# Memory attention in a decoder step: values products one step later, cached values in the weight ring, decode chain over steps 8 to 16

## The chip, the cores and the metric

The kernel runs on one core of one Trainium2 chip. The metric is the device time of one execution in microseconds. A core has the engines PE (TensorE, matrix products), DVE (VectorE), ACT (ScalarE), POOL (GpSimd) and SP (SyncE, which here only issues transfers). Each engine has its own instruction list and works it off in order; engines meet at semaphores alone. So a wait holds up everything behind it on the same engine.

## What is computed

One step of a hybrid decoder layer, for 512 prompt tokens and 8 sequences with 4 new tokens each (32 decode tokens, 544 columns in all), width 1024, all in fp32. The layer is a mixer (a state space part beside differential attention), then cross-attention into 256 memory tokens, then a SwiGLU FFN. The part that matters here is the cross-attention with 4 heads of 256:

```python
def mem_attend(hn, mk, mv, w_mq, w_mo):
    q = (hn @ w_mq).reshape(b, t, N_MEM_HEADS, MEM_HEAD_DIM)
    s = jnp.einsum("bqhd,bkhd->bhqk", q, mk)
    p = jax.nn.softmax(s * (MEM_HEAD_DIM ** -0.5), axis=-1)
    o = jnp.einsum("bhqk,bkhd->bqhd", p, mv).reshape(b, t, D_MODEL)
    return o @ w_mo
```

It runs twice: for the prompt with keys and values made from `mem_prompt`, and for the decode tokens with `cache_mem_k` and `cache_mem_v`, 8 sequences of 256 x 1024 each, 1 MB per sequence for keys and 1 MB for values.

## The kernel before

**Weights.** Each weight matrix is cut into units of 1 MB (1024 x 256), numbered through the kernel: U_MQ = 21 to 24 is `w_mq`, U_MO = 25 to 28 is `w_mo`, U_FFN = 29. A product is made of three passes on high and low parts, so a unit goes through three two-slot buffers, slot n % 2: SP loads it to `w_raw`, ACT copies the high part to `w_hi` (`split_hi`, waits for the load and for the last product that read unit n - 2), POOL subtracts to `w_lo` (`split_lo`). SP's `ahead(n)` issues all loads up to unit n that are still missing; ACT's `hi_ahead(n)` does the same for the high parts. Each load waits for the low part of unit n - 2.

**The memory stage.** `mem_order` (lines 405 to 419) is one list that PE, ACT and DVE each walk, every engine doing its share of each entry. It has 18 steps. In step n:
- `ma n`: scores of head n // 4 for the token tile n % 4. PE makes four products (L2125), DVE the maximum (L1570, L1571), ACT the exp (L946), DVE the reciprocal and scaling of tile n - 1 (L1553, L1554).
- `mt n-2` (`ma_tail`): PE transposes the tile's weights (L1797), ACT copies them to `m_pT` (L729). Behind the fourth tile of a head, `ma_tail` on PE waits for that copy and makes the head's values product (L2113, eight products of 512 columns), which `mo h` (`ma_out`, L1563) on DVE turns into high and low parts.
- `kt`, `ks` (steps 0 to 8): sixteen blocks of cached keys, each with 8 transposes into PSUM banks 2 and 7, two copies to `dm_kT` on ACT (L954, L956) and 8 small products (L2144).
- the decode chain: `dsm` and `dsc` (softmax on DVE and ACT), `dpt` (transposes, copy to `dm_pT` L1589), `dv 0` and `dv 1` (cached values products for sequences 0 to 3 and 4 to 7, L2159, into banks 2 and 7), `do` (ACT copies them to `dm_o`, L965), `dot` (transposes and four DVE operations).

**Orders around it.** Ahead of `mem_order`, ACT runs `for n_ in range(4): hi_ahead(U_MQ + n_ + 1)`, so up to unit 25; behind it, `hi_ahead(U_MO + 1)`, unit 26. Behind it, PE runs 16 half products of `w_mo` (`half_product`, L1777) in the order of `HALF_ORDER`: four tiles over the first 272 columns, the same four over the last 272 (which hold the decode tokens), then the other four tiles.

**Buffers of the cached keys and values.** Keys 0 to 3 go to `kv_slots` 0 to 3, keys 4 to 7 to `kx_slots`, which lie on `x_hi` and `x_lo` and are free once unit 24's products are done. Values 0 to 3 reuse `kv_slots` 0 to 3, value 4 has slot 4, value 5 slot 5 (the place of `dm_qz`), values 6 and 7 slots 0 and 1 again.

Of the kernel before, what the change touches and what calls it, by code (L numbers as in the profile page):

```python
# [13 lines left out]
F32 = mybir.dt.float32  # L14
# [6 lines left out]
P = 128  # L21
D = 1024
# [9 lines left out]
NMEM, MH, MD = 256, 4, 256  # L32
# [48 lines left out]
def build(nc, A, O):  # L81
# [123 lines left out]
    kv_slots = [at(f"dm_kv{i}", [P, 2, D], F32, C0 + off) for i, off in enumerate((61440, 69632, 77824, 25600, 33792, 86016))]  # L205
    kx_slots = [at(f"dm_kx{i}", [P, 2, D], F32, B0 + i * 8192) for i in range(4)]
    dm_k = kv_slots[:4] + kx_slots
    dm_v = kv_slots[:4] + kv_slots[4:6] + kv_slots[:2]
    mkT = at("mkT", [P, KT, NMEM], F32, C0 + 45056)
    mv_tok = at("mv_tok", [P, 2, D], F32, C0 + 53248)  # L210
    mk_tok = at("mk_tok", [P, 2, D], F32, C0 + 34816)
# [16 lines left out]
    def bank(i):  # L228

        return pall[:, i, :]  # L230
# [172 lines left out]


    mem_order = []
    for n in range(len(MATT) + 2):
        if n < 16:
            mem_order.append(("ma", n))
        if n < 8:
            mem_order.append(("kt", 2 * n))  # L410
            if n:
                mem_order.append(("ks", 2 * n - 1))
            mem_order += [("kt", 2 * n + 1), ("ks", 2 * n)]
        mem_order += {8: [("ks", 15), ("dsm", 0), ("mo", 0)], 9: [("dsc", 0)], 10: [("dpt", 0), ("mo", 1)], 11: [("dv", 0)],
                      12: [("do", 0)], 13: [("dv", 1), ("dot", 0), ("dot", 1)], 14: [("do", 1), ("mo", 2)],
                      15: [("dot", 2), ("dot", 3)], 16: [("mtail", 15)]}.get(n, [])
        if n >= 2:
            mem_order.append(("mt", n - 2))
    mem_order.append(("mo", 3))

    w_loaded = [S("w_loaded0"), S("w_loaded1")]
    w_hi_ready, w_lo_ready = S("w_hi_ready"), S("w_lo_ready")
# [10 lines left out]
    def _(sp_eng):  # L433
# [135 lines left out]
            e.dma_start(dm_k[b][:], mk_view[b]).then_inc(S("kv_in0"), 16)  # L569
        e.wait_ge(S("mk_stored"), 16)  # L570
        e.dma_start(dm_v[4][:], mv_view[4]).then_inc(S("kv_in3"), 16)
        ahead(U_MO + 1)
        e.wait_ge(acc_full, used(U_MO - 1))
        for b in range(4, 8):
            e.dma_start(dm_k[b][:], mk_view[b]).then_inc(S("kv_in1"), 16)
        e.wait_ge(S("dmT_pe"), 16)
        for b in range(4):
            e.dma_start(dm_v[b][:], mv_view[b]).then_inc(S("kv_in2"), 16)
        e.wait_ge(S("dms"), 16)
        e.dma_start(dm_v[5][:], mv_view[5]).then_inc(S("kv_in3"), 16)  # L580
        e.wait_ge(S("dm_pv"), 1)
        for b in range(6, 8):
            e.dma_start(dm_v[b][:], mv_view[b]).then_inc(S("kv_in3"), 16)
        ahead(U_FFN - 3)

        gate = A["w_gate"][0].rearrange("(k p) c -> p k c", p=P)
# [30 lines left out]
    @block.gpsimd  # L617
    def _(pool):
        e = pool

        def split_lo(n, kts, cols, i=None, per=0):

            off = 0 if i is None else i * per
            e.wait_ge(w_hi_ready, off + (n + 1))
            w = kts * cols
            e.tensor_tensor(w_lo[:, n % 2, 0:w], w_raw[:, n % 2, 0:w], w_hi[:, n % 2, 0:w].bitcast(F32), ALU.subtract)\  # L626
                .then_inc(w_lo_ready, 1)

        e.memset(c_out[:], 0.0).then_inc(S("zeroed"), 1)
        e.memset(c_pad[:], 0.0).then_inc(S("zeroed"), 1)  # L630
        e.wait_ge(S("xs_ready"), 5)
        e.memset(b_pad[:], 0.0).then_inc(S("zeroed"), 1)

        e.wait_ge(w_lo_ready, U_MQ + 1)
        for n in range(U_MQ + 1, U_FFN):
            split_lo(n, *units[n][1:])
        e.wait_ge(w_lo_ready, U_FFN + 1)
        with e.Fori(0, PAIRS - 1) as i:
            for s_ in range(1, 3):
                split_lo(U_FFN + s_, KT, 256, i, 2)  # L640
        for n in range(U_DOWN + 1, N_UNITS):
            split_lo(n, DOWN_K[(n - U_DOWN) % 3][1], 256)
# [3 lines left out]
    def _(act):  # L646
# [294 lines left out]
        for kind, n in mem_order:  # L941
            if kind == "ma":
                e.wait_ge(S("ma_max"), n + 1)
                if n >= 4:
                    e.wait_ge(S("ma_pT"), n - 3)
                e.activation(m_p[:, n % 4, :], bank(4 + n % 2)[:, 0:NMEM], ACT.Exp, scale=MD ** -0.5,  # L946
                             bias=small[:, 28 + n % 4:29 + n % 4], accum_out=small[:, 32 + n % 4:33 + n % 4]).then_inc(S("ma_exp"), 1)
            elif kind == "mt":
                ma_tail(n)
            elif kind == "kt":  # L950
                e.wait_ge(S("dmT_pe"), 2 * n + 1)
                if n >= 2:
                    e.wait_ge(S("dms"), n - 1)
                e.activation(dm_kT[n % 2][:, 0:2, :], bank(2).rearrange("p (a b) -> p a b", a=2), ACT.Copy).then_inc(S("dmT_out"), 1)  # L954
                e.wait_ge(S("dmT_pe"), 2 * n + 2)
                e.activation(dm_kT[n % 2][:, 2:4, :], bank(7).rearrange("p (a b) -> p a b", a=2), ACT.Copy).then_inc(S("dmT_out"), 1)  # L956
            elif kind == "dsm":
                e.wait_ge(S("dm_max"), 1)
                for t in range(2):
                    e.activation(dm_p[:, t, :], bank(3)[:, t * NMEM:(t + 1) * NMEM], ACT.Exp, scale=MD ** -0.5,  # L960
                                 bias=small[:, D_NM + t:D_NM + t + 1], accum_out=small[:, D_L + t:D_L + t + 1]).then_inc(S("dm_exp"), 1)
            elif kind == "do":
                e.wait_ge(S("dm_pv"), n + 1)
                for g in range(2):
                    e.activation(dm_o[:, n, g * 512:(g + 1) * 512], bank((2, 7)[g]), ACT.Copy).then_inc(S("dmo_out"), 1)  # L965
# [31 lines left out]
                e.wait_ge(*n4_add_after((n - 4) // 8, (n - 4) % 8))  # L997
            e.activation(q4_half[:, n % 4, :], yT[:, k, in_half(a)], ACT.Square, scale=D ** -0.5).then_inc(S("norm_sq"), 1)

        hi_ahead(U_MO + 1)  # L1000
        for i in range(13):
            evac_half(i)
            if i == 3:
# [740 lines left out]
    def _(pe):  # L1744
# [355 lines left out]
        def ma_tail(n):  # L2100
            h, i = MATT[n]
            e.wait_ge(S("ma_p"), n + 1)
            if n >= 1:
                e.wait_ge(S("ma_pTo"), n)
            transposes(bank(6), [m_p[:, n % 4, k * P:(k + 1) * P] for k in range(2)]).then_inc(S("ma_pT"), 1)
            if i == 3:
                e.wait_ge(S("ma_pTo"), n + 1)
                for d in range(2):
                    if 0 < h < 3:
                        e.wait_ge(S("ma_o"), 2 * (h - 1) + d + 1)  # L2110
                    for k in range(2):
                        c = (2 * h + d) * P
                        ins = mm(bank(d if h < 3 else 4 + d), mv_tok[:, k, c:c + P], m_pT[:, k, :], start=k == 0, stop=k == 1)  # L2113
                    ins.then_inc(S("ma_pv"), 1)


        e.wait_ge(S("mk_tok_ready"), 4)
        for kind, n in mem_order:
# [7 lines left out]
                ins.then_inc(S("ma_s"), 1)  # L2126
            elif kind == "mt":
                ma_tail(n)
            elif kind == "kt":
                t, k = n // KT, n % KT  # L2130
                if k == 0:
# [34 lines left out]
                    e.wait_ge(S("dmx"), 2 * n)  # L2166
                transposes(bank(3), [dm_o[:, t, k * P:(k + 1) * P] for k in range(4 * half, 4 * half + 4)]).then_inc(S("dmoT"), 1)

        e.wait_ge(S("dmx"), 8)
        def sum_half(out, name, a):  # L2170

            e.wait_ge(*counted(name, "add", 7 * (a + 1)) if name == "n4" else counted("n3", "add", 14 if a else half_adds(11)))
# [13 lines left out]
        def during_mo(i):  # L2186

            def at_k(k):
                if i == 0:
                    e.wait_ge(S("ma_o"), max(6, k + 1))  # L2190
                if (i, k) == (12, 4):
                    sum_half(bank(4), "n3", 0)
                if (i, k) == (13, 2):
                    rows_half(bank(4), "n3", 0)
            return at_k
# [108 lines left out]
```

## Time and profile before

| what | value |
|---|---|
| median of 3 runs | 1030.5 us (1030.44 to 1030.97) |
| the profiled execution, its own time | 1034.07 us |
| its span | 1032.2 us |
| mean granted clock of PE | 0.959 |
| PE busy | 938.9 us, 91% |
| DVE, ACT, POOL busy | 444.8, 362.8, 179.4 us |
| the chain that ended last, by engine | PE 81%, DVE 9%, ACT 5%, issue 3% |

The page cuts the span into 40 slices of 25.8 us; the stage lies in slices 18 to 22 (counted from 1). Each digit is a share in tenths:

```profile
PE   1999989787789999999869989999999999999997
PEclk9999999878789999999988989999999999999999
DMA  7214105422142156745161201222223222222212
```

Busy time of PE is a modelled one, and a busy PE at half clock does half the work, so the rows PE and PEclk have to be read together.

### The profile page before, as it was taken

Reading aid. Unit: us, or ns where it says so; the run is one execution under the profiler, and the core shown is the slowest. Engines: PE = TensorE matmul, PEld = TensorE weight load, DVE = VectorE, ACT = ScalarE, POOL = GpSimd, SP = SyncE. Lnnn points to the kernel's source line nnn. Section 1 sums busy time; section 2 is a strip of 40 time slices with the busy share of each in tenths; the row PEclk is TensorE's granted clock in tenths of the full one; section 3 lists DMA queues with packets and bytes.
Section 4 is the critical chain, followed back from the end, with each engine's and each line's share of the span. In section 5 each row is a group of like instructions: output and inputs, shape, how many; then the busy total and the mean of one; then the engine's idle time right before and its main releaser. Section 6 shows DMA issues by size and latency. Waiting matters only on the chain.

```text
span 1032.2 us, 17627 instructions
## 1 busy us (share of the span) xinstructions
PE 938.9 (91%) x7480; PEld 858.2 (83%) x7480; DVE 444.8 (43%) x895; ACT 362.8 (35%) x570; POOL 179.4 (17%) x45
## 2 busy tenths in 40 slices
PE   1999989787789999999869989999999999999997
PEld 1899987663369998985427979999999999999997
DVE  2699984664634488111432556322222222101013
ACT  5423223664345365135322454322222322122121
POOL 3000000000000001310001300344433334333330
PEclk9999999878789999999988989999999999999999
DMA  7214105422142156745161201222223222222212
GB/s 208 90 42 123 60 25 190 160 75 90 41 168 81 57 176 219 286 156 211 42 203 42 82 2 42 82 81 81 81 86 107 91 81 81 91 94 72 83 31 87
DMA packets 85341, 105.82 MB, mean 103 GB/s; under 512 B 9473, under 2 KB 72834, under 8 KB 85154
## 3 DMA queue, kind: packets, MB, share of 16 engines
q1 hardware_dynamic: 85282, 104.97, 30.8%
q8 instruction: 45, 0.74, 0.3%
q14 instruction: 14, 0.11, 0.0%
HBM read 98.26 MB, written 6.70 MB: 102 GB/s over the span
## 4 chain that ended last, share of the span: by engine, by line
PE 81%; DVE 9%; ACT 5%; issue 3%; DMA 1%; POOL 1%; SPq 0%; DVEq 0%; ACTq 0%
PE pall L1765 55%; PE pall L1777 6%; PE pall L1797 4%; PE pall L2073 2%; PE pall L2113 2%; ACT w_hi L663 1%; PE pall L2159 1%; DVE w_lo L1088 1%; PE pall L1847 1%; PE pall L2125 1%; PE pall L1950 1%; PE pall L1941 1%; PE pall L1830 1%; PE pall L1851 1%; DVE a_s L1406 1%
## 5 line engine op out<-in xcount | busy, mean ns | idle before, releaser
L626 POOL TENSOR_TENSOR w_lo<-w_raw,w_hi 128x2048 fp32r<-128x2048 f32 (+1 forms) x38 | 171.3, 4508 | 807.2 <-ACT w_hi L663 423.2
L1765 PE MATMUL pall<-x_hi,w_hi 128*128 128x272 f32 x1024 | 214.2, 291 | 2.9 <-DVE x_lo L1148 1.6
L1765 PE MATMUL pall<-x_lo,w_hi 128*128 128x272 f32 x1024 | 212.6, 289 | 0.0
L1765 PE MATMUL pall<-x_hi,w_lo 128*128 128x272 f32 x1024 | 211.4, 288 | 0.0
L1765 PEld LDWEIGHTS pall<-x_hi,w_hi 128*128 128x128 f32 x1024 | 160.9, 189 | 4.4 <-issue 1.9
L1765 PEld LDWEIGHTS pall<-x_lo,w_hi 128*128 128x128 f32 x1024 | 162.1, 190 | 0.0
L1765 PEld LDWEIGHTS pall<-x_hi,w_lo 128*128 128x128 f32 x1024 | 161.4, 189 | 0.0
L663 ACT ACTIVATE w_hi<-w_raw 128x2048 fp32r<-128x2048 f32 (+1 forms) x61 | 114.7, 1880 | 101.4 <-PE pall L1765 101.3
L1765 PE MATMUL pall<-g_hi,w_hi 128*128 128x272 f32 x352 | 73.1, 289 | 0.0
L1765 PE MATMUL pall<-g_lo,w_hi 128*128 128x272 f32 x352 | 72.6, 288 | 0.0
L1765 PE MATMUL pall<-g_hi,w_lo 128*128 128x272 f32 x352 | 72.6, 287 | 0.0
L1088 DVE TENSOR_TENSOR w_lo<-w_raw,w_hi 128x2048 fp32r<-128x2048 f32 x23 | 52.7, 2290 | 19.3 <-ACT w_hi L663 19.2
L1082 DVE TENSOR_TENSOR sq<-pall,rstd 128x544 f32<-128x544 f32 (+1 forms) x24 | 16.1, 676 | 91.5 <-PE pall L1765 87.8
L1765 PEld LDWEIGHTS pall<-g_lo,w_hi 128*128 128x128 f32 x352 | 55.3, 189 | 0.0
L1765 PEld LDWEIGHTS pall<-g_hi,w_hi 128*128 128x128 f32 x352 | 55.1, 188 | 0.0
L1765 PEld LDWEIGHTS pall<-g_hi,w_lo 128*128 128x128 f32 x352 | 55.1, 189 | 0.0
L1082 DVE TENSOR_TENSOR tt<-pall,rstd 128x544 f32<-128x544 f32 (+1 forms) x24 | 16.0, 676 | 83.6 <-PE pall L1765 80.4
L1085 DVE TENSOR_TENSOR sqacc<-sqacc,sq 128x544 f32<-128x544 f32 x20 | 17.1, 853 | 77.1 <-ACT sq L696 76.3
L1050 ACT ACTIVATE g_hi<-sq 128x544 f32 x20 | 13.2, 659 | 98.2 <-DVE sq L1082 98.2
L1046 ACT ACTIVATE tt<-tt 128x544 f32<-128x544 f32 x20 | 13.2, 659 | 79.3 <-DVE tt L1082 79.3
L1777 PE MATMUL pall<-x_hi,w_hi 128*128 128x272 f32 x128 | 38.3, 299 | 1.9 <-POOL w_lo L626 1.9
L1777 PE MATMUL pall<-x_hi,w_lo 128*128 128x272 f32 x128 | 37.6, 294 | 0.0
(373 smaller groups left out, 1609.8 us busy)
## 6 DMA issues: line engine op xcount, KB each, us to landing
w_raw<-in_w_gate SPq DMA_DIRECT2D x10, 1024.0 KB, 5.3
w_raw<-in_w_up SPq DMA_DIRECT2D x10, 1024.0 KB, 5.3
w_raw<-in_w_in SPq DMA_DIRECT2D x8, 1024.0 KB, 5.9
dm_kv<-in_cache_mem_v SPq DMA_DIRECT2D x8, 1024.0 KB, 7.2
w_raw<-in_w_down SPq DMA_DIRECT2D x8, 1024.0 KB, 5.0
w_raw<-in_w_out SPq DMA_DIRECT2D x4, 1024.0 KB, 8.6
d_k<-in_cache_k SPq DMA_DIRECT2D x16, 256.0 KB, 3.3
d_v<-in_cache_v SPq DMA_DIRECT2D x16, 256.0 KB, 3.9
```

Source lines behind the costliest of these rows:

```text
L626: e.tensor_tensor(w_lo[:, n % 2, 0:w], w_raw[:, n % 2, 0:w], w_hi[:, n % 2, 0:w].bitcast(F32), ALU.subtract)\
L663: e.activation(w_hi[:, n % 2, 0:w], w_raw[:, n % 2, 0:w], ACT.Copy).then_inc(w_hi_ready, 1)
L1046: e.activation(tt[:, m, :], tt[:, m, :], ACT.Silu).then_inc(S("silu"), 1)
L1050: e.activation(g_hi[:, bass.ds(i * 2 + (m + 2), 1), :], sq[:, m:m + 1, :], ACT.Copy).then_inc(S("g_hi_ready"), 1)
L1082: return e.tensor_tensor(out, a, b, ALU.mult)
L1085: return e.tensor_tensor(out, a, b, ALU.add)
L1088: return e.tensor_tensor(out, a, b, ALU.subtract)
L1765: ins = mm(acc(j)[:, a, :], w, x[:, k_x + k, a * HALF:(a + 1) * HALF], start=first and k == 0 and s_, stop=last and k == kts - 1 and t_)
L1777: ins = mm(out[:, 0:HALF], w, x[:, k, in_half(a)], start=k == 0 and s_, stop=k == KT - 1 and t_)
L1797: ins = e.transpose(dst[0:src.shape[1], at_:at_ + w], src, ident[0:w, 0:w])
L2073: ins = mm(out, l, r, start=k == 0 and i == 0, stop=k == KT - 1 and i == 2)
L2113: ins = mm(bank(d if h < 3 else 4 + d), mv_tok[:, k, c:c + P], m_pT[:, k, :], start=k == 0, stop=k == 1)
```

## The change

- PE's values products leave `ma_tail` and become entries `mv h` of their own, in step 4h + 6, behind that step's `ma` and ahead of its `kt` entries (the last one behind step 17).
- The values 5, 6 and 7 get the buffers `w_lo` slot 0, `w_lo` slot 1 and `w_hi` slot 0 and are loaded right behind the keys 4 to 7. In return POOL's low part of unit 25 and ACT's high part of unit 26 wait for `dm_pv` 2, the end of `dv 1`; unit 26's high part becomes the entry `next_hi` in step 15.
- On SP, `ahead(U_MO + 1)` in front of the loads of keys 4 to 7 becomes `ahead(U_MO)` behind them.
- The decode chain's entries are set on other steps, and the wait for its last part (`dmx` 8) goes from the end of the memory order to the fifth half product.

```diff
-    dm_v = kv_slots[:4] + kv_slots[4:6] + kv_slots[:2]
+    dm_v = kv_slots[:5] + [at(f"dm_vw{i}", [P, 2, D], F32, off) for i, off in enumerate((W_LO, W_LO + 8192, W_HI))]
@@ mem_order
+    beside_scores = {8: [("ks", 15), ("dsm", 0), ("mo", 0)], 9: [("dsc", 0)], 10: [("dpt", 0)], 11: [("dv", 0), ("mo", 1)], 12: [("dv", 1)],
+                     13: [("dot", 0)], 14: [("dot", 1)], 15: [("dot", 2), ("mo", 2)], 16: [("mtail", 15), ("dot", 3)]}
     for n in range(len(MATT) + 2):
+        if n in (12, 13):
+            mem_order.append(("do", n - 12))
         if n < 16:
             mem_order.append(("ma", n))
+        if n % 4 == 2 and n > 4:
+            mem_order.append(("mv", n // 4 - 1))
         if n < 8:
             mem_order.append(("kt", 2 * n))
             if n:
                 mem_order.append(("ks", 2 * n - 1))
             mem_order += [("kt", 2 * n + 1), ("ks", 2 * n)]
-        mem_order += {8: [("ks", 15), ("dsm", 0), ("mo", 0)], 9: [("dsc", 0)], 10: [("dpt", 0), ("mo", 1)], 11: [("dv", 0)],
-                      12: [("do", 0)], 13: [("dv", 1), ("dot", 0), ("dot", 1)], 14: [("do", 1), ("mo", 2)],
-                      15: [("dot", 2), ("dot", 3)], 16: [("mtail", 15)]}.get(n, [])
+        mem_order += beside_scores.get(n, [])
         if n >= 2:
             mem_order.append(("mt", n - 2))
-    mem_order.append(("mo", 3))
+        if n == 15:
+            mem_order.append(("next_hi", 0))
+    mem_order += [("mv", MH - 1), ("mo", MH - 1)]
@@ SP
         e.dma_start(dm_v[4][:], mv_view[4]).then_inc(S("kv_in3"), 16)
-        ahead(U_MO + 1)
         e.wait_ge(acc_full, used(U_MO - 1))
         for b in range(4, 8):
             e.dma_start(dm_k[b][:], mk_view[b]).then_inc(S("kv_in1"), 16)
+        ahead(U_MO)
+        for b in range(5, 8):
+            e.dma_start(dm_v[b][:], mv_view[b]).then_inc(S("kv_in3"), 16)
         e.wait_ge(S("dmT_pe"), 16)
         for b in range(4):
             e.dma_start(dm_v[b][:], mv_view[b]).then_inc(S("kv_in2"), 16)
-        e.wait_ge(S("dms"), 16)
-        e.dma_start(dm_v[5][:], mv_view[5]).then_inc(S("kv_in3"), 16)
-        e.wait_ge(S("dm_pv"), 1)
-        for b in range(6, 8):
-            e.dma_start(dm_v[b][:], mv_view[b]).then_inc(S("kv_in3"), 16)
         ahead(U_FFN - 3)
@@ POOL
         for n in range(U_MQ + 1, U_FFN):
+            if n == U_MO:
+                e.wait_ge(S("dm_pv"), 2)
             split_lo(n, *units[n][1:])
@@ ACT
+            elif kind == "next_hi":
+                e.wait_ge(S("dm_pv"), 2)
+                hi_ahead(U_MO + 1)
...
-        hi_ahead(U_MO + 1)
         for i in range(13):
             evac_half(i)
@@ PE
-            if i == 3:
-                e.wait_ge(S("ma_pTo"), n + 1)
-                for d in range(2):
...
+        def ma_values(h):
+
+            e.wait_ge(S("ma_pTo"), 4 * h + 4)
+            for d in range(2):
...
+            elif kind == "mv":
+                ma_values(n)
...
-        e.wait_ge(S("dmx"), 8)
...
+                if (i, k) == (4, 0):
+                    e.wait_ge(S("dmx"), 8)
```

## Rows read from the trace of the kernel before

**Rows 1.** Windows: us; busy of PE, PEld, DVE, ACT, POOL; PEclk; DMA; GB/s.
```profile
473.00:497.00 24.00, 22.13 (x172) 13.61 (x171) 4.01 (x16) 12.91 (x30) 0.00 (x0) 1.00 0.46 175
497.00:512.00 15.00, 11.18 (x44) 6.09 (x44) 7.39 (x22) 3.93 (x15) 0.00 (x0) 0.89 0.21 72
517.00:530.00 13.00, 7.66 (x43) 2.62 (x41) 2.00 (x8) 2.27 (x7) 0.00 (x0) 0.74 0.45 159
540.00:554.00 14.00, 9.93 (x26) 5.25 (x27) 5.35 (x18) 3.51 (x6) 4.51 (x1) 0.63 0.02 5
```

**Rows 2.** Waits of PE, 455 to 560: total us, times, longest.
```profile
PE pall L2159 <- DMA dm_kv<-in_cache_mem_v: 5.3, 1, 5.3
```

**Rows 3.** Chain that ended last: start, us, what.
```profile
504.19 5.40 PE pall L2113 x8
512.21 3.69 PE pall L2159 x32
523.52 6.02 PE pall L2159 x32
546.90 6.34 PE pall L2113 x8
553.25 24.09 PE pall L1777 x192
```

**Rows 4.** Windows, two single microseconds.
```profile
528.00:529.00 1.00, 1.00 (x14) 0.13 (x4) 0.00 (x0) 0.00 (x0) 0.00 (x0) 0.82 0.00 0
552.00:553.00 1.00, 1.00 (x4) 0.42 (x2) 0.14 (x1) 0.00 (x0) 1.00 (x1) 0.87 0.00 0
```

**Rows 5.** Timeline of SP's queue: start, us, what.
```profile
426.23 12.39 SPq L440 DMA_DIRECT2D w_raw<-in_w_mo  x2
455.62 2.34 SPq L575 DMA_DIRECT2D dm_kx<-in_cache_mem_k  x4
```

**Rows 6.** Timeline of ACT around the stage's start.
```profile
443.66 1.92 ACT L663 ACTIVATE w_hi<-w_raw 128x2048 fp32r<-128x2048 f32 x1 [10.11 <-PE pall L1765]
445.60 1.28 ACT L946 ACT_TABLE_LOAD   x1
457.14 0.47 ACT L946 ACTIVATE m_p<-pall,small 128x256 f32<-128x256 f32 x1 [10.26 <-DVE small L1571]
```

**Rows 7.** The four transfers into dm_kx, issue to landing.
```profile
DMA to landing us min/median/max: 5.1/8.2/12.8
```

**Rows 8.** Windows, while these transfers run.
```profile
459.00:461.00 2.00, 2.00 (x18) 1.27 (x17) 0.00 (x0) 1.03 (x2) 0.00 (x0) 1.00 1.03 424
```

**Rows 9.** Timeline of PE, first transposes of step 1.
```profile
458.25 1.15 PE L1797 MATMUL pall<-ident,dm_kv 128*128 128x128 f32 x8 [0.68 <-ACT dm_kT L954]
```

**Rows 10.** Timeline of ACT, another table load.
```profile
596.27 1.28 ACT L979 ACT_TABLE_LOAD   x1
597.56 0.26 ACT L979 ACTIVATE small<-pall,small 68x4 f32<-68x4 f32 x1
```

**Rows 11.** Chain, steps 4 to 6.
```profile
476.85 1.14 PE pall L1797 x8
481.59 1.14 PE pall L1797 x8
487.84 0.88 PE pall L2125 x4
490.50 1.14 PE pall L1797 x8
```

**Rows 12.** Lines, 455 to 553.3: busy us, mean ns | idle.
```profile
L1563 DVE CAST x_hi<-pall 128x512 fp32r<-128x512 f32 x8 | 5.5, 686 | 7.1 <-PE pall L2113 7.1
L965 ACT ACTIVATE dm_o<-pall 128x512 f32<-128x512 f32 x4 | 2.1, 592 | 0.0
```

**Rows 13.** Timeline, steps 9 and 10.
```profile
502.66 0.41 DVE L1570 TENSOR_REDUCE small<-pall 128x1 f32<-128x256 f32 x1
503.76 0.37 ACT L729 ACTIVATE m_pT<-pall 128x256 f32<-128x256 f32 x1
```

More of the change, by code:

```diff
@@ L2105, in ma_tail @@
             transposes(bank(6), [m_p[:, n % 4, k * P:(k + 1) * P] for k in range(2)]).then_inc(S("ma_pT"), 1)
-            if i == 3:
-                e.wait_ge(S("ma_pTo"), n + 1)
-                for d in range(2):
[L2109 to L2114, printed above, removed]
+        def ma_values(h):
+            e.wait_ge(S("ma_pTo"), 4 * h + 4)
+            for d in range(2):
+                if 0 < h < 3:
+                    e.wait_ge(S("ma_o"), 2 * (h - 1) + d + 1)
+                for k in range(2):
+                    c = (2 * h + d) * P
+                    ins = mm(bank(d if h < 3 else 4 + d), mv_tok[:, k, c:c + P], m_pT[:, k, :], start=k == 0, stop=k == 1)
+                ins.then_inc(S("ma_pv"), 1)
         e.wait_ge(S("mk_tok_ready"), 4)
```

## The prediction

> **What bounds the kernel now.** I read the page first: PE is busy for 91% of the span and carries 81% of the chain that ended last, so nothing is gained where PE is dense; only PE's gaps and its slow clock are for sale. The change touches one stage, memory attention (PE from 455.3 us to the first output product at 553.25 us). The page's slices show the granted clock below full there, so next I read the window table [rows 1]. From 473 to 497 us (steps 4 to 7) PE is busy for 22.1 of 24 us at full clock. Behind that it is busy for 11.2 of 15, 7.7 of 13 and 9.9 of 14 us, at a granted clock of 0.89, 0.74 and 0.63 (a mix of 1.2 and 2.4 GHz). The waits name the longest single wait, 5.3 us for a transfer of cached values [rows 2]. The chain gives the dates [rows 3]: values product of head 1 at 504.19, cached values product 0 at 512.21 and 1 at 523.52, values product of head 3 at 546.90, output product at 553.25. After the gap that ends at 523.52, PE runs at half clock until late in 528; after the thin stretch before 546.90 until late in 552 [rows 4]. The values product takes 5.40 and 6.34 us there.
>
> **What is added: a load that ACT waits for.** The diff changes the loads' order too. Before, SP issues units 25 and 26 (w_mo) from 426.23 [rows 5], and ACT makes w_hi of 25 at 443.66 [rows 6]. After, SP waits for the last product of MQ, issues the four dm_kx loads (455.62 to 457.96 [rows 5]), and only then unit 25, with three value loads behind it. ACT's code still makes w_hi of 25 ahead of the whole memory order (`hi_ahead(U_MQ + n_ + 1)`, n_ = 3). Queued behind that wait on ACT are the exp table load, every softmax exp, every copy of transposed keys, and through these copies PE's bank 2 and 7: after ma 0 and the first eight transposes PE has nothing that it may do.
>
> How long: the first dm_kx transfer lands 5.1 us after issue, 460.7, the last 12.8 us after issue, near 469.9 [rows 7]; at 424 GB/s [rows 8] each MB takes 2.5 us, so they land one behind the other. Unit 25 is the fifth MB: 470.8 (460.7 plus four times 2.5) to 472.4 (469.9 plus 2.5). I take 471.6. Then w_hi 1.92, table load 1.28 and the small gaps: first exp at 474.9, where it now starts at 457.14 [rows 6]. The stall is **17.7 us** (16.8 to 18.8). PE takes up work not at 458.25 [rows 9] but at 476, after 18 us of nothing, so at half clock. The trace shows how that ends: resumed at 523.52, full speed back near 528.2 [rows 3, 4], 4.7 us at half rate, 2.35 us of work lost. Here a step has about 0.35 us of slack, so **2.0 us** (1.2 to 2.4).
>
> On the table load: the trace shows the next activation 0.01 us behind the end of a 1.28 us load [rows 10]. The Trainium skill (ScalarE: Activation LUTs, "What ACT_TABLE_LOAD costs") adds a drain of about 1.38 us to each switch; by that the stall would be an estimated 19.1 us. No row shows such a drain, and the sum goes without it.
>
> **What moves in steps 5 and 6.** Now values product 0 sits between the scores of steps 5 and 6 and waits for its copy. The chain has 4.74 us between second transposes (476.85, 481.59) but 8.91 over step 6 (481.59 to 490.50) [rows 11]: the product adds 4.17 for about 3.5 us of PE work. After, ma 6 goes ahead, and its reduce, exp and the copies run beside the product. The 0.4 us copy wait and most of the 0.35 us wait for ACT go: **1.0 us** (0.6 to 1.2).
>
> **Steps 8 to 17, redone by hand.** Durations: scores 0.88 [rows 11], cached values product 3.7 at full clock [rows 3], the others as below.
> - Steps 8 and 9 keep their order: DVE's softmax reduction for decode and ma_out 0 (four 0.69 us operations [rows 12]) end at 502.66, the reduce of ma 9 runs there, and ACT's copy at 503.76 [rows 13] still releases values product 1 at 504.19. Only ma 10 slips ahead. The product stays at 5.4 us if the clock falls as now: 509.6. dpt, mt 8 and ma 11 take 1.5: cached values 0 starts at 511.0, not 512.21, since DVE's copy no longer lags.
> - It ends at 514.7. mt 9 and ma 12 follow; cached values 1 waits for ACT to copy banks 2 and 7 out: one m_pT copy 0.4 and two of 0.59 less their overlap, 1.1 [rows 12]. Start 516.3. Its data landed by about 480 (seven loads and one of weights behind 455.62, 2.5 us each), so the 5.3 us wait and the half clock behind it go. End 519.9.
> - mt 10, ma 13, dot 0, mt 11, ma 14: 2.6, values product 2 at 522.5, for 3.5. dot 1, mt 12, ma 15: 1.6, 527.6.
> - Now DVE ends last: reduce and tail 1.1, dot 2's four small operations 0.8, ma_out 2 2.75, the last tail 0.5: 532.7. mt 15 and its copy: values product 3 starts at 533.2, not 546.90. **13.7 us** gained; if the clock doesn't fall before values product 1, 15.3; with one more copy or wait in each of three steps, 12.
> - Values product 3 follows a thin stretch (528 to 533) like today's, so it stays near half clock: 6.0 for 6.34, **0.3 us** (up to 2.6 if the clock holds).
> Edits at nothing: w_hi of 26 (1.9 us on ACT, ahead of mt 14's copy) lies beside ma_out 2's 2.75 us; uncovered it costs 1.9. w_lo of 25 on POOL now waits for cached values 1 and has over 10 us before the output product. The wx loads come earlier; w_raw of 27 and 28 wait for hi and lo slots that output halves free, so PE's later gaps don't change. The dm_v loads 0 to 3 queue behind landed ones.
>
> **Sum.** +17.7 +2.0 -1.0 -13.7 -0.3 = +4.7 us. The profiled execution took 1034.07 us for a span of 1032.2; it would give 1036.9 of span. The shown runs have their median at 1030.5, 3.6 below the profiled one; the difference carries over: **1035.2 us**. With all terms at their ends: 16.8+1.2-1.2-15.3-2.6 = -1.1, and 18.8+2.4-0.6-12 = +8.6: 1029.4 to 1039.1.
>
> **The rivals.**
> - *Faster: unit 25 lands early.* If its transfer doesn't stand behind the four dm_kx loads, the stall shrinks. The balance tips at a landing of 466.9 us (15.0 us of gain less 2.0 of clock, less 3.3 for w_hi and table, from 457.14). In second place, 463.3, it gives -3.6: 1026.9. Against it: landings spread from 5.1 to 12.8 us [rows 7], which is one after another. 6%.
> - *The other way: the three value loads share with unit 25.* Then it lands as late as the eighth MB, 478.2 to 480: +7.5, 1042.7. Rows 7 speak against that as well, but not for transfers of unequal row length. 8%.
> - *The clock doesn't come back among key transposes.* Steps 1 to 7 hold 16 transposes each beside few long products. Today they run at full clock [rows 1], but they start warm. At half clock a step of 4.74 becomes about 8.2: +3.5 in each of up to seven steps, less the 2.0 counted, +22: 1057; after two more steps 1042. The Trainium skill (TensorE: Matmul & The Clock Gate, "PE-mode transpose") says that transposes don't count as busy work for the clock; by it this is the case to fear, though the trace holds full clock through the 24 us of this mix in rows 1. 12%.
> - *The chain doesn't thin.* If the clock also falls between steps 12 and 15, those 11 us of dense work lose 2.4 per fall: 1040. 7%.
> - *The change does less than it says:* values 5 to 7 are late all the same, since SP issues them behind the stall. They are issued by 460 and ACT isn't in their way, so 2%, +8.
>
> **How the numbers follow.** Forecast (terms within their ends) 65%: of it 55 slower by over 0.2% (2.1 us, about what a measurement of this kernel can tell from no change), 8 within, 2 faster. The other slower cases add 29, the early landing 6 to faster. Faster 0.08, same 0.08, slower 0.84. The range reaches from 1030 (the near end of the forecast, since all lucky ends at once are rare) to 1043, which takes in the sharing loads and the weaker clock case, and leaves out the stuck clock and the early landing.
>
> **What would show it.** Right: PE idle from about 457.6 to 476 with ACT's w_hi near 471.6 ahead of the first exp; half clock behind it; no wait of the cached values product for a transfer; 7.9 us between the second transposes over step 6 with its product; the distance from the first exp after the stall to the output product down from 96 to about 83 us. Wrong: w_hi of 25 before 467; a PE gap under 10 us; a clock of 0.5 beyond 485; cached values 1 more than 2 us behind cached values 0's end; values product 3 less than 12 us earlier against step 8, whose scores start at 497.2.

## The result: 10.9 us slower

The changed kernel takes 1041.5 us (median of 4 runs, 1037.98 to 1042.45) against 1030.7 us before. The ratio is 1.0098, with a 95% interval from 1.0078 to 1.0119. The sign and the place of the loss were forecast, and the time lies inside the stated range, but the forecast change was +4.7 us: the loss came in full and the gain in good part did not.

Page of the changed kernel, span and slices:

```profile
span 1040.1 us, 17628 instructions
PE   1999988787799999957897989999999999999997
PEclk9999999977799999988988989999999999999999
```

Slices 18 and 19 (PE 5 and 7 tenths, where the kernel before had 9 and 9) hold a hole that was not there. The window table, with the columns of rows 1: the hole, the recovery behind it, and stretches that answer to those of rows 1.

```profile
457.00:473.00 16.00, 0.00 (x0) 0.00 (x0) 0.00 (x0) 4.00 (x5) 0.00 (x0) 0.53 1.04 402
473.00:479.00 6.00, 5.71 (x28) 4.08 (x28) 0.65 (x3) 1.96 (x5) 0.00 (x0) 0.56 0.50 199
486.00:510.00 24.00, 22.95 (x181) 14.96 (x174) 4.44 (x17) 12.95 (x30) 0.00 (x0) 1.00 0.59 219
528.00:541.00 13.00, 12.27 (x90) 5.62 (x89) 6.77 (x16) 4.70 (x13) 3.42 (x1) 1.00 0.17 49
541.00:561.00 20.00, 12.95 (x40) 6.54 (x40) 13.15 (x33) 4.25 (x9) 5.60 (x2) 0.74 0.56 179
```

PE does nothing for 16 us, ACT little, and the transfer engines run at 402 GB/s: everyone waits for SP's queue. Then 6 us mostly at half clock. The key steps (486 to 510) are as dense as in rows 1. The stretch of the cached values products (528 to 541) is busy for 12.3 of 13 us at full clock, where rows 1 had 7.7 of 13 at 0.74: that part of the change works. The end (541 to 561) is thin and slow like that of rows 1.

PE's waits in the stage, answering to rows 2 (total us, times, longest):

```profile
PE pall L1805 <- ACT dm_kT L960: 20.1, 7, 18.1
PE pall L1805 <- DVE m_p L1562: 5.4, 1, 5.4
```

The transfer is gone from this list. In its place stand 18.1 us for ACT's copy of keys, and 5.4 us for a scaling on DVE. The load in the chain that ended last (start, us, what):

```profile
455.58 13.37 DMA w_raw<-in_w_mo
```

ACT in order of time, in brackets the idle time before an instruction and what ended it:

```profile
468.97 1.91 ACT L669 ACTIVATE w_hi<-w_raw 128x2048 fp32r<-128x2048 f32 x1 [37.80 <-DMA w_raw<-in_w_mo]
470.89 1.28 ACT L952 ACT_TABLE_LOAD   x1
472.19 0.47 ACT L952 ACTIVATE m_p<-pall,small 128x256 f32<-128x256 f32 x1
```

SP issues the four key loads, then unit 25's; that one lands 13.37 us later; ACT makes `w_hi` from it, loads its table, makes the first exp and the first copy; PE goes on. Rows 6 had the same three ACT instructions at 443.66, 445.60 and 457.14, two of them under the MQ products. For the second wait, DVE in order of time:

```profile
539.47 2.78 DVE L1562 TENSOR_SCALAR m_p<-m_p,small 128x256 f32<-128x256 f32 x1
...
550.02 3.54 DVE L1562 TENSOR_SCALAR m_p<-m_p,small 128x256 f32<-128x256 f32 x1
```

And POOL:

```profile
537.58 4.53 POOL L630 TENSOR_TENSOR w_lo<-w_raw,w_hi 128x2048 fp32r<-128x2048 f32 x1 [101.73 <-PE pall L2170]
548.91 4.50 POOL L630 TENSOR_TENSOR w_lo<-w_raw,w_hi 128x2048 fp32r<-128x2048 f32 x1 [6.81 <-ACT w_hi L669]
```

The same instruction, 128 x 256 from SBUF to SBUF, takes 0.35 us alone and 2.78 or 3.54 beside POOL's subtraction. It ends at 542.25 and 553.56, POOL at 542.11 and 553.41.

The chain, answering to rows 3 (values products 1 and 3):

```profile
520.25 6.58 PE pall L2123 x8
...
554.77 6.38 PE pall L2123 x8
```

**The account.** To compare stages I set both traces to the issue of the first key load (455.62 before, 453.24 after) and take the start of the scores of step 8 and of the first output product. The profiled executions differ ahead of the stage too. That is not the change's: a second execution of the kernel before issues these loads at 453.40 (e8_before_again).

| from the key loads' issue to | before | after | difference |
|---|---|---|---|
| first exp | 1.52 | 18.95 | +17.4 |
| scores of step 8 (497.15; 513.22) | 41.53 | 59.98 | +18.5 |
| first output product (552.68; 560.59) | 97.06 | 107.35 | +10.3 |

So the stage explains 10.3 us of the 10.9. From step 8 on it is 8.2 us shorter (55.53 to 47.37), not the 14.0 that I had counted.

### The profile page after: what moved, and what is told of

Its sections match the earlier page's. It is cut to its first block, busy times and chain, and to the rows that moved or that the text cites. A ratio compares the mean times of both kernels' runs of the same rounds, so it can differ in the third digit from the quotient of the medians.

```text
span 1040.1 us, 17628 instructions
## 1 busy us (share of the span) xinstructions
PE 934.4 (90%) x7480; PEld 855.3 (82%) x7480; DVE 450.4 (43%) x895; ACT 363.3 (35%) x570; POOL 179.4 (17%) x45
## 4 chain that ended last, share of the span: by engine, by line
PE 79%; DVE 10%; ACT 5%; issue 3%; DMA 2%; POOL 1%; SPq 0%; DVEq 0%; ACTq 0%
PE pall L1773 53%; PE pall L1785 6%; PE pall L1805 3%; PE pall L2081 2%; PE pall L2123 2%; DMA w_raw<-in_w_mo 1%; ACT w_hi L669 1%; DVE w_lo L1096 1%; PE pall L2134 1%; PE pall L1855 1%; PE pall L1958 1%; PE pall L1949 1%; PE pall L1838 1%; PE pall L1859 1%; DVE a_s L1414 1%
```

## The experiments

Theory 1: the whole loss is the place of unit 25's load. Rival A: the mass of loads queued together. Theory 2, formed on the trace after: POOL's subtraction keeps DVE's scaling out, and ate part of the gain. Rival B: the long scaling is DVE's own affair.

### The load alone, taken back and put in

e1_load_first moves the call back:

```diff
+        ahead(U_MO)
         e.wait_ge(acc_full, used(U_MO - 1))
         for b in range(4, 8):
             e.dma_start(dm_k[b][:], mk_view[b]).then_inc(S("kv_in1"), 16)
-        ahead(U_MO)
```

> The changed kernel with one line moved: SP issues the load of unit 25 where the kernel before did, ahead of its wait for the last MQ product, and not behind the four key loads. Theory 1 (ACT's wait for this load is the whole stall at the start of the stage: w_hi of 25 at 468.97, the first exp at 472.19, PE idle 18.1 us): the stall of 17.4 us and about 1 to 2 us of half clock behind it go, so 1041.5 falls to about 1023 (1021 to 1025), and w_hi of 25 is made while the third MQ unit's successor runs, some 10 us ahead of the first exp. Rival A (the keys and values that are now queued together hold the stage up, and the load is only the last of them): PE still waits at the start, and less than 5 us comes back.

Measured: 1018.0 us (1017.5 to 1022.0), ratio 0.9873 (0.9844 to 0.9903) to the kernel before, which took 1032.3 beside it and 1030.7 beside the changed kernel of the result. ACT in order of time:

```profile
440.54 1.92 ACT L669 ACTIVATE w_hi<-w_raw 128x2048 fp32r<-128x2048 f32 x1 [10.11 <-PE pall L1773]
442.48 1.28 ACT L952 ACT_TABLE_LOAD   x1
454.02 0.47 ACT L952 ACTIVATE m_p<-pall,small 128x256 f32<-128x256 f32 x1 [10.26 <-DVE small L1579]
```

PE's wait for the copies of keys (total us, times, longest):

```profile
PE pall L1805 <- ACT dm_kT L960: 2.8, 7, 0.7
```

`w_hi` of unit 25 is back under the MQ products, and PE's wait for the copies of keys falls from 20.1 us in total to 2.8, although the three value loads still stand in the queue behind the keys. Theory 1 holds and rival A falls. What came back is 23.5 us, though, more than the 16.5 to 20.5 expected (23.3 us of it within the stage by the traces); the part about the clock below takes that up.

e2_late_load is the kernel before with that alone:

```diff
-        ahead(U_MO + 1)
         e.wait_ge(acc_full, used(U_MO - 1))
         for b in range(4, 8):
             e.dma_start(dm_k[b][:], mk_view[b]).then_inc(S("kv_in1"), 16)
+        ahead(U_MO + 1)
```

> The kernel before with one line moved the other way: the loads of units 25 and 26 are issued behind the loads of keys 4 to 7. Nothing else of the change is in it. Theory 1: the same stall, 17.4 us, and 1 to 2.4 us of half clock behind it: 1030.7 becomes about 1049.5 (1047 to 1051). Rival A: under 5 us more.

Measured: 1053.1 us (1052.6 to 1054.0) against 1032.3, ratio 1.0205 (1.0184 to 1.0227), +20.8 us. That is 2.0 more than the +18.8 expected, and the time lies above the expected 1047 to 1051. The stage in its trace takes 115.7 us for 97.1, +18.6. Another 1.8 us lie behind the stage (481.3 us from the first output product to the end, for 479.5), and no run says why.

ACT's `w_hi` of unit 25 in order of time:

```profile
469.57 1.91 ACT L663 ACTIVATE w_hi<-w_raw 128x2048 fp32r<-128x2048 f32 x1 [37.84 <-DMA w_raw<-in_w_mo]
```

PE's wait for ACT's copies of keys:

```profile
PE pall L1797 <- ACT dm_kT L954: 20.5, 8, 18.2
```

The same hole, 18.2 us, in a kernel that has nothing else of the change. Up to the scores of step 8 it costs 19.7 us (61.2 for 41.5); from there on this kernel is 1.0 us shorter (54.5 for 55.5), since its last values product takes 4.90 us, not 6.34, though cached values product 1 takes 6.49, not 6.02.

### POOL beside DVE

e3_hi_behind moves `("next_hi", 0)` from step 15 to the end of the memory order, so that POOL's subtraction of unit 26 comes after the last scaling:

```diff
-        if n == 15:
-            mem_order.append(("next_hi", 0))
+    mem_order.append(("next_hi", 0))
     mem_order += [("mv", MH - 1), ("mo", MH - 1)]
```

> The changed kernel with the high part of unit 26 (the entry next_hi) behind the last transposes of the memory order instead of in step 15. Theory 2 (while POOL subtracts the low part of a unit, DVE's scaling of m_p, which reads and writes SBUF alone, doesn't get through: 3.54 us instead of 0.35, and it ends with POOL's 4.5 us): POOL's subtraction of unit 26 then comes behind the last scaling, which takes 0.35 us again, and the last values product starts about 3.2 us earlier: 1038.3 (1037.5 to 1039.5). Rival B (the long scaling is DVE's own, or a wait for ACT's high part): the time stays within 1 us of 1041.5, or rises by ACT's 1.9 us.

Measured: 1037.1 us (1034.2 to 1039.7), 4.4 less than the changed kernel, which ran at another time, and 0.4 under the expected range. The part of it that is the edit's is read from the trace. DVE's scalings in its trace:

```profile
537.84 2.78 DVE L1561 TENSOR_SCALAR m_p<-m_p,small 128x256 f32<-128x256 f32 x1
...
548.38 0.35 DVE L1561 TENSOR_SCALAR m_p<-m_p,small 128x256 f32<-128x256 f32 x1
```

PE's transposes behind the last one:

```profile
548.79 0.69 PE L1804 MATMUL pall<-ident,m_p 128*128 128x128 f32 x2 [2.16 <-DVE m_p L1561]
```

The last scaling is 0.35 us again and PE's wait for it 2.2 instead of 5.4; from the scores of step 8 to the output product it is 44.1 us instead of 47.4, 3.3 less, as priced. The edit also moves ACT's 1.9 us for the high part of unit 26, but that is not what helps: the last scaling starts at the same place, 36.8 us behind the scores of step 8, in both kernels, and only its length differs. The earlier one, beside unit 25's subtraction, is still 2.78: PE is inside values product 2 then and doesn't miss it.

e4_pool_beside puts the contention into the key steps of the kernel before, where there was none:

```diff
         for n in range(U_MQ + 1, U_FFN):
+            if n == U_MO + 1:
+                for i, step in enumerate((2, 4, 6)):
+                    e.wait_ge(S("dmT_pe"), 4 * step)
+                    if i:
+                        e.wait_ge(S("extra"), i)
+                    e.tensor_tensor(w_lo[:, 0, :], w_raw[:, 1, :], w_hi[:, 1, :].bitcast(F32), ALU.subtract).then_inc(S("extra"), 1)
+                e.wait_ge(S("extra"), 3)
             split_lo(n, *units[n][1:])
```

> The kernel before with three more subtractions on POOL (128 x 2048, 4.5 us each, from SBUF into a free slot of w_lo) beside steps 2, 4 and 6 of the memory order, where POOL is otherwise idle. Nothing waits for their result. Theory 2: in these stretches DVE's scaling of m_p (SBUF to SBUF) grows from 0.35 us to as much as 4.5 and ends with POOL's instruction, while its reads of PSUM keep their 0.42 us; DVE's list is held up and the steps beside are longer, 3 to 10 us in all. Rival B: no DVE instruction changes, and the time stays at 1030.7.

The cut leaves out one line, by which SP's later loads of weights wait for the three subtractions. The first two of them, in order of time:

```profile
463.44 4.54 POOL L642 TENSOR_TENSOR w_lo<-w_raw,w_hi 128x2048 fp32r<-128x2048 f32 x1 [13.78 <-PE pall L1805]
472.74 4.55 POOL L642 TENSOR_TENSOR w_lo<-w_raw,w_hi 128x2048 fp32r<-128x2048 f32 x1 [4.76 <-PE pall L1805]
```

DVE in the same time:

```profile
465.02 0.42 DVE L1578 TENSOR_REDUCE small<-pall 128x1 f32<-128x256 f32 x1 [3.49 <-PE pall L2133]
...
465.74 2.38 DVE L1562 TENSOR_SCALAR m_p<-m_p,small 128x256 f32<-128x256 f32 x1
...
475.22 2.22 DVE L1562 TENSOR_SCALAR m_p<-m_p,small 128x256 f32<-128x256 f32 x1
```

Both scalings that meet a subtraction grow, to 2.38 and 2.22 us, and end at 468.12 and 477.44, where POOL ends at 467.98 and 477.29. The maxima in the same microseconds, which read PSUM, keep 0.42. The third subtraction (482.21 to 486.72) meets no scaling. Rival B falls. The time doesn't move (1032.5 against 1032.3, ratio 0.9997, 0.9987 to 1.0008), so the 3 to 10 us that I expected with it were wrong: in the key steps nobody waits for the scaling. The same DVE delay costs 0 us there and 3.3 at the end of the stage.

### Both repairs, and DVE's order

e5_first_and_hi is the changed kernel with the edits of e1_load_first and e3_hi_behind together:

```diff
+        ahead(U_MO)
         e.wait_ge(acc_full, used(U_MO - 1))
...
-        ahead(U_MO)
...
-        if n == 15:
-            mem_order.append(("next_hi", 0))
+    mem_order.append(("next_hi", 0))
```

> Both repairs on the changed kernel: unit 25's load issued where it was before, and unit 26's high part behind the memory order. Alone they gave 1018.0 and 1037.1 against 1041.5. Theory (two separate losses: ACT's wait for the load, and POOL's subtraction beside DVE's last scaling): they add up, 1018.0 less 3.2 to 4.4, about 1014 (1013 to 1015.5). Rival (they overlap, or the clock takes the gain back because PE's thin stretch is shorter and the half clock then lies on the output products): 1016.5 to 1018.

Measured: 1015.5 us (1013.2 to 1017.1), ratio 0.9824 (0.98 to 0.9848). The range touches the expected 1013 to 1015.5 and the runs scatter by 4 us, so the times alone do not tell adding from overlapping; the traces do: from the scores of step 8 to the output product 43.8 us in e1_load_first, 40.1 here, 3.7 less.

e6_order is e5_first_and_hi with two of DVE's `ma_out` entries (`mo` 0 and 2) one step later:

```diff
-    beside_scores = {8: [("ks", 15), ("dsm", 0), ("mo", 0)], 9: [("dsc", 0)], 10: [("dpt", 0)], 11: [("dv", 0), ("mo", 1)], 12: [("dv", 1)],
-                     13: [("dot", 0)], 14: [("dot", 1)], 15: [("dot", 2), ("mo", 2)], 16: [("mtail", 15), ("dot", 3)]}
+    beside_scores = {8: [("ks", 15), ("dsm", 0)], 9: [("mo", 0), ("dsc", 0)], 10: [("dpt", 0)], 11: [("dv", 0), ("mo", 1)], 12: [("dv", 1)],
+                     13: [("dot", 0)], 14: [("dot", 1)], 15: [("dot", 2)], 16: [("mtail", 15), ("mo", 2), ("dot", 3)]}
```

> The kernel of e5_first_and_hi with three of DVE's entries moved: ma_out 0 from step 8 to step 9, behind the scores of step 9; the last softmax tail ahead of ma_out 2; the last dot behind it. Theory 3 (PE's two gaps that are left, 1.6 and 1.2 us ahead of values product 1 and some 3 to 5 us ahead of values product 3, are DVE doing the four 0.69 us operations of ma_out first): values product 1 starts about 1.5 us earlier in its step, values product 3 about 2.7 us earlier, and if the gaps get too short for the clock to fall, up to 2 us more at each: 1010 (1007 to 1011.5). Rival (ma_out is needed as early as it stands, so it only changes places with what it delayed): within 1 us of e5_first_and_hi.

Measured: 1012.0 us (1010.1 to 1013.4), ratio to the kernel before 0.9801 (0.9782 to 0.982). That is 3.6 us less than e5_first_and_hi, of the 5.5 expected.

Two of PE's waits, at an output product and at the values products:

```profile
PE pall L1784 <- POOL w_lo L629: 1.3, 1, 1.3
...
PE pall L2122 <- ACT m_pT L734: 0.5, 1, 0.5
```

And the last values product in order of time:

```profile
523.70 5.40 PE L2122 MATMUL pall<-m_pT,mv_tok 128*128 128x512 f32 x8 [0.47 <-ACT m_pT L734]
```

The 1.2 us wait ahead of values product 1 is gone. The last product still runs mostly at half clock (5.40 us for 3.7), so the 2 us that I hoped for from the clock there did not come. From the scores of step 8 to the output product it is 36.8 us, against 40.1 in e5_first_and_hi. The wait of 1.3 us for POOL's `w_lo` is no price of the late `next_hi`. It comes at 554.54, 26.0 us behind the first output product, and the changed kernel has it in the same place:

```profile
586.60 0.39 PE L1785 MATMUL pall<-x_hi,w_hi 128*128 128x272 f32 x1 [1.32 <-POOL w_lo L630]
```

The kernel before has it too, at 578.64. From the first output product to the end it is 479.5 us before and after the change and 479.8 here, so `next_hi` behind the memory order costs at most 0.3 us there. This is the fastest version of the study, 20.1 us below the kernel before that ran beside it (1032.1).

### The parts of the change by themselves

e7_values_later is the kernel before with `ma_values` and the `mv` entries alone (PE's part, the same as in the change, is left out of the cut):

```diff
+        if n % 4 == 2 and n > 4:
+            mem_order.append(("mv", n // 4 - 1))
...
-    mem_order.append(("mo", 3))
+    mem_order += [("mv", 3), ("mo", 3)]
```

> The kernel before with the values products one step later, and nothing else of the change. The prediction's reading: 1.0 us at step 6, about 0.9 at step 10 since one set of scores goes ahead of the product, little in step 14, where the wait for the cached values comes first: 2 to 3 us less than the kernel before. Rival: ACT's copies and the transfer set the end of those steps and nothing changes (within 0.5 us).

Measured: 1023.1 us (1021.1 to 1024.3), ratio 0.9903 (0.988 to 0.9926): 9.0 us, three times what I expected. From the key loads' issue to step 8 the trace gives 1.2 us, and from there to the output product 8.0 (47.6 for 55.6).

Values product 1 and cached values product 1 in order of time:

```profile
500.49 3.70 PE L2117 MATMUL pall<-m_pT,mv_tok 128*128 128x512 f32 x8 [1.34 <-ACT m_pT L731]
...
516.80 6.46 PE L2165 MATMUL pall<-dm_kv,dm_pT 128*32 128x512 f32 x32 [5.20 <-DMA dm_kv<-in_cache_mem_v]
```

Values product 1 takes 3.70 us, not 5.40 as in rows 3: the clock doesn't fall ahead of it. The transfer is still waited for, for 5.2 us. What stands behind it is closer together: from cached values product 1 to values product 3 it is 19.6 us instead of 23.4. The scores of step 14 now go ahead of values product 2; that they are the reason is read from the order, not tested. Counted from step 8, cached values 0 and 1 start 2.9 and 3.0 us earlier, values product 3 6.8, the output product 8.0. Rival: falls.

e9_ring_alone has only the three buffers and their loads, with the waits of POOL and ACT that go with them, and unit 25's load left early:

```diff
-    dm_v = kv_slots[:4] + kv_slots[4:6] + kv_slots[:2]
+    dm_v = kv_slots[:5] + [at(f"dm_vw{i}", [P, 2, D], F32, off) for i, off in enumerate((W_LO, W_LO + 8192, W_HI))]
...
+        for b in range(5, 8):
+            e.dma_start(dm_v[b][:], mv_view[b]).then_inc(S("kv_in3"), 16)
...
+            if n == U_MO:
+                e.wait_ge(S("dm_pv"), 2)
...
+        e.wait_ge(S("dm_pv"), 2)
```

> The kernel before with nothing of the change but the place of values 5 to 7 (two free slots of w_lo and one of w_hi), their loads right behind keys 4 to 7, and the low part of unit 25 behind the second cached values product. Unit 25's load stays early. The prediction's reading: the 5.3 us wait for the transfer goes, and the half clock behind that gap with it (2 to 2.4 us of lost work); POOL's subtraction now lies beside one or two of DVE's scalings (up to 3 us, of which the last values product feels little): 6 to 8 us less than the kernel before. Rival: ACT's copies out of banks 2 and 7 come when the transfer does, so another wait ends there: under 3 us less.

Measured: 1026.6 us (1024.2 to 1028.1) against 1032.8, ratio 0.9942 (0.9922 to 0.9962), 6.2 us.

PE's longest wait at the cached values products:

```profile
PE pall L2159 <- ACT dm_o L964: 1.3, 1, 1.3
```

The transfer's 5.3 us are gone and a wait of 1.3 for ACT's copies out of banks 2 and 7 stands in their place: cached values product 1 starts 4.1 us earlier against step 8 (22.3 for 26.4), not 5.3. The half clock behind the gap goes too. Rival: right in kind, small in size. 9.0 and 6.2 make 15.2 us for the two parts. All of the change but the late load (e1_load_first) gives 14.3, with 3.3 lost to POOL, so 17.6 without that loss. The third part, the decode chain's new order, is in neither run and wasn't run by itself; the 2.4 us between are the chain's and what the parts do for each other, which these runs don't tell apart.

### The clock, by two second traces

e8_before_again is the kernel before, unchanged:

> The kernel before, unchanged, for a second trace. The trace that the prediction was made from is of an execution of 1034.07 us, with the median at 1030.5. Reading 1: executions differ in where the clock falls, so this trace has its half-clock microseconds in other places or fewer of them, while the order and the durations at full clock are the same; stages without a change of clock take the same time within 0.3 us. Reading 2: the profiled execution is longer evenly, by 0.35% everywhere.

The execution took 1031.91 us, its span 1030.1 against 1032.2. A window ahead of the stage, with the columns of rows 1, in the trace of the prediction:

```profile
180.00:225.00 45.00, 36.12 (x234) 30.61 (x234) 29.01 (x81) 28.78 (x55) 0.00 (x0) 0.73 0.35 120
```

And in this one:

```profile
180.00:225.00 45.00, 36.32 (x238) 29.47 (x237) 29.16 (x82) 30.39 (x60) 0.00 (x0) 0.77 0.36 119
```

From step 8 to the output product it is 55.5 us there and 55.6 here; the clock ahead of the stage is 0.73 there and 0.77 here. So reading 1 fits: where an execution is longer it spends more time at 1.2 GHz in stages with gaps; two traces don't prove it.

e10_change_again is the changed kernel, unchanged:

> The changed kernel, unchanged, for a second trace. Its first trace has half clock from the gap ahead of values product 1 on (6.6 us for the product), the traces of e1_load_first, e5_first_and_hi and e7_values_later don't (3.7 us), although PE's gaps there are the same 1.6 and 1.2 to 1.3 us. Reading 1: whether the clock falls at this gap differs from execution to execution, and this trace may show either. Reading 2: it falls always when the stall at the stage's start has come before. In both readings the last scaling of DVE again ends with POOL's subtraction (3.5 us), and the stall is again 17 to 18 us.

1041.6 us. The stage repeats to 0.1 us (47.4 from step 8 to the output product), the scaling too (3.54), and the stall is 17.3 us.

Values product 1 in this trace, in order of time:

```profile
519.89 6.62 PE L2123 MATMUL pall<-m_pT,mv_tok 128*128 128x512 f32 x8 [1.35 <-ACT m_pT L735]
```

And in that of e1_load_first:

```profile
499.87 3.70 PE L2123 MATMUL pall<-m_pT,mv_tok 128*128 128x512 f32 x8 [1.25 <-ACT m_pT L735]
```

Both kernels have the same gaps of 1.6 and about 1.3 us ahead of this product; with the stall it takes 6.6 us, without it 3.7. That is so in three traces with the stall (changed kernel twice, e3_hi_behind) and in three without (e1_load_first, e5_first_and_hi, e7_values_later). So reading 2 fits in this order of entries: with the stall there are 2.9 us of half clock more, some 45 us behind it. The 23.3 us that the stage of e1_load_first is shorter (84.1 for 107.4) are 19.7 up to step 8, these 2.9, and 0.7 at the last values product (5.64 for 6.38). But no rule follows. In the order of before, the same product takes 5.40 us without the stall and 5.40 with it (e2_late_load), behind a longer gap of 2.2 us in both, and there the last product is shorter with the stall. Why the clock falls at the gap of 1.3 us in the one case only stays open: an accident of timing that repeats with each kernel would look the same.

## Why the prediction was right or wrong

**The late load: right.** Stall 17.7 us forecast, 17.4 measured; landing of unit 25 471.6 in the frame of the first trace, 468.95 measured, which is 471.3 there; first in, first out held. Half clock behind it 2.0 forecast, 2.2 measured (19.65 us from e1_load_first to the changed kernel at step 8, less 17.43). The Trainium skill's drain of 1.38 us behind a table load (ScalarE: Activation LUTs, "What ACT_TABLE_LOAD costs") isn't there: the exp comes 0.02 us behind the load.

**Steps 5 and 6: right.** 1.0 us forecast, 1.2 measured (41.53 to 40.33 in e1_load_first).

**Steps 8 to 17: this step failed.** 13.7 and 0.3 us of gain forecast, 8.2 measured. These 5.8 us are most of the 6.2 by which the forecast change was too small. In order of size:
- 3.3 us: the sentence "w_lo of 25 on POOL ... has over 10 us" and the one on w_hi of 26, both in the list of "edits at nothing"; the low part of unit 26, which does the harm, isn't in it at all. I asked whether POOL's result comes in time, and not whom POOL's instruction keeps out while it runs. `next_hi` in step 15 releases POOL at 548.91, 1.1 us ahead of the one scaling that the stage's end waits for (e3_hi_behind, e4_pool_beside). The rule stood in the Trainium skill (SBUF — State Buffer, "SBUF: two separate sides"): a GpSimd operation, and a VectorE one in a two-port mode or with two inputs in SBUF, take one pair of ports by an exclusive lock for a whole instruction, and the one that starts second waits. The rows agree: each of the four scalings ends 0.14 to 0.15 us behind POOL.
- 1.2 us: values product 1 priced at 5.40 us, its duration before; it took 6.58, at half clock for longer.
- 0.3 us: I gave the last product 0.3 us less half clock; it had none less.
- 1.0 us: small pieces of the hand schedule. With the scores of step 8 set on 497.15, cached values 0 starts at 512.2 for the 511.0 forecast (the 1.2 us above), cached values 1 at 517.8 for 516.3, values product 2 at 524.2 for 522.5 and values product 3 at 538.7 for 533.2. So 0.3 and 0.2 us came on the way to values product 2, and about 0.5 beside POOL's 3.3 behind it.

No row of before had the two side by side in this stage, but the same trace had them just behind it, and the prediction doesn't use it:

```profile
574.01 4.58 POOL L626 TENSOR_TENSOR w_lo<-w_raw,w_hi 128x2048 fp32r<-128x2048 f32 x1 [20.77 <-ACT w_hi L663]
574.79 4.10 DVE L1085 TENSOR_TENSOR sqacc<-sqacc,q_half 128x272 f32<-128x272 f32 x1 [2.50 <-ACT q_half L973]
```

DVE's sum takes 0.44 us at 565.77 with POOL idle, and here 4.10, to 0.3 us behind POOL's end. So engines do not meet at semaphores alone, as the section on the cores had it: these two also meet where both work in SBUF.

Without POOL in the way and with the clock of e5_first_and_hi the same stretch is 40.1 us, a gain of 15.4. With values product 1 at the 5.40 us of the forecast and not at 3.70 it would be 13.7, for the 14.0 forecast: the order itself was read well.

**The baseline: right by luck of place.** The excess of the first profiled execution lay ahead of the stage (e8_before_again), so the difference did carry over to the median.

**The rivals.** *Early landing* fell: 13.37 us from issue to landing. *Sharing with the value loads* fell: unit 25, the fifth load, landed at 468.95 with the three value loads queued behind it, and the eighth had been put at 478.2, which is 475.8 in this frame. *The clock that doesn't come back among key transposes* fell: PE resumed at 473.29, the clock was still 0.50 in 477 to 478 and 0.86 in 478 to 479, and the key steps ran at 1.00 (486 to 510). The Trainium skill's sentence that transposes don't count as busy work (TensorE: Matmul & The Clock Gate, "PE-mode transpose") isn't borne out by this mix of transposes, scores and small products. *The chain that doesn't thin* fell: the clock was full from 528 until 549, past the scores of step 15 (544.48). *Values 5 to 7 late all the same* fell: PE has no wait for a transfer at the cached values, though SP was done issuing them at 464.0 and not by 460. The true rival, one engine kept waiting by another with which it shares nothing in the program, wasn't among them; the 84% for slower and the upper end of 1043 held only since other mishaps had been given room; the terms of the sum themselves reached to 1039.1, and the time was 1041.5.

## What to carry to other kernels

When a load is moved in SP's queue, look for the instruction that consumes it on every engine and for what is queued behind that instruction: here one line of order cost 23 us and hid a change worth 14, and e1_load_first shows that the rest of the change was good. When work is moved to or released on POOL, list DVE's SBUF-to-SBUF operations in that time, and ask if one of them is on the path: the same delay was free in the key steps and cost 3.3 us at the end. Test a change of several parts part by part before it is judged by its sum.

## What the runs showed of the hardware

- DVE's scaling of 128 x 256 fp32 in SBUF takes 0.35 us alone and waits for the end of a POOL subtraction that has begun (2.2 to 3.5 us here, four cases), while DVE's maxima out of PSUM beside it keep their 0.42 us. A sum of two SBUF inputs waits in the same way (4.10 us for 0.44, in the kernel before).
- Of the loads of 1 MB queued on SP, the first of the keys lands 5.0 us after its issue and the fifth load 13.4 us after its own (15.7 us behind the first issue), while the engines move about 400 to 424 GB/s: one behind the other.
- After 18 us without work PE ran at 1.2 GHz from 473.3 us until within the microsecond from 478 (granted clock 0.50, then 0.86 in that one) and then at 2.4 GHz, although most of that work was transposes and small products.
- Two traced executions of the kernel before differ by 2.1 us of span and in the granted clock ahead of the stage (0.73 and 0.77 from 180 to 225 us), not in the stage from step 8 on (0.1 us).
